# One decoder layer on one core: order of the late value rows, of the last one-hot batches and of four TensorE rows changed

## The reference, cut to what matters

```python
xs  = h.reshape(n_chunks, 128, D)          # two chunks of 128 tokens
idx = expert_idx.reshape(n_chunks, 128, K) # K = 8 heads * 16 experts of 128 * 128
u   = jnp.take(expert_u, ic, axis=0)
act = gelu(einsum('ckd,cd->ck', u, xc))
vv  = jnp.take(expert_v, ic, axis=0)
out = einsum('ck,ckd->cd', gc * act, vv)   # then h + out, and an RMS norm over D
```

## Time and profile before

| | us |
|---|---|
| median of 3 runs | 2041.2 (2039.21 to 2043.6) |
| the profiled execution, its own time | 2039.45 |
| its span, first to last instruction | 2037.5 |
| TensorE busy | 1788.4 (88%) |
| VectorE busy | 1368.4 (67%) |
| GpSimd busy | 1022.5 (50%) |
| ScalarE busy | 560.0 (27%) |

### The profile page before, as it was taken

One profiled execution on the slowest core, in us unless ns is written; L12 is line 12 of the kernel. 1 busy time (PEld: TensorE's weight loads), 2 busy tenths in 40 slices (PEclk: granted clock), 3 DMA queues, 4 the chain that ended last, 5 costly groups with the idle time before them and its releaser, 6 DMA issues.

```text
span 2037.5 us, 21513 instructions
## 1 busy us (share of the span) xinstructions
PE 1788.4 (88%) x7530; PEld 1188.6 (58%) x7531; DVE 1368.4 (67%) x2205; ACT 560.0 (27%) x1011; POOL 1022.5 (50%) x643
## 2 busy tenths in 40 slices
PE   7999999999999999765565578888877989999997
PEld 7998899888998898622222233444433544444442
DVE  4473453223324348899999988887888877888866
ACT  5334453345433520201010033223314620000001
POOL 4443343444332414566655554564555656777742
PEclk9999999999999999877777899999998999999998
DMA  8875454655546689999999999999999989999997
GB/s 208 239 174 147 141 184 155 197 190 186 167 145 198 194 287 399 344 421 418 417 418 415 410 402 398 402 416 402 404 417 401 397 302 403 385 410 378 397 421 318
DMA packets 157650, 647.41 MB, mean 318 GB/s; under 512 B 25894, under 2 KB 31086, under 8 KB 95598
## 3 DMA queue, kind: packets, MB, share of 16 engines
q0 software_dynamic: 73728, 450.98, 54.7%
q1 hardware_dynamic: 83824, 195.16, 29.5%
HBM read 729.91 MB, written 2.10 MB: 359 GB/s over the span
## 4 chain that ended last, share of the span: by engine, by line
PE 61%; DMA 18%; DVE 14%; issue 4%; POOL 2%; ACT 0%; DVEq 0%; POOLq 0%; SPq 0%; ACTq 0%
PE acc L1813 8%; PE misc L1813 8%; DMA u_ring<-in_peer_u_dram,idx 7%; DMA v_high<-in_peer_v_dram,idx 7%; PE acc L1469 5%; PE acc L1471 5%; PE acc L1470 5%; PE acc L1476 5%; PE acc L1477 5%; PE acc L1478 5%; DVE product L1314 5%; DVE product L1316 5%; PE misc L1778 4%; PE acc L1758 3%; DMA v_low<-in_peer_v_dram,idx 1%
## 5 line engine op out<-in xcount | busy, mean ns | idle before, releaser
L486 POOL TENSOR_TENSOR w_lo<-raw,w_hi 128x1024 fp32r<-128x1024 f32 x112 | 273.4, 2441 | 430.0 <-ACT w_hi L583 429.6
L1778 PE MATMUL misc<-v_high,diag 128*128 128x512 f32 x512 | 268.1, 673 | 104.9 <-DMA v_high<-in_peer_v_dram,idx 96.9
L1778 PE MATMUL misc<-v_low,diag 128*128 128x512 f32 x512 | 274.0, 688 | 93.5 <-DMA v_low<-in_peer_v_dram,idx 77.6
L583 ACT ACTIVATE w_hi<-raw 128x1024 fp32r<-128x1024 f32 x224 | 237.0, 1060 | 352.7 <-PE acc L1478 171.5
L910 DVE TENSOR_TENSOR w_lo<-raw,w_hi 128x1024 fp32r<-128x1024 f32 x112 | 149.3, 1334 | 266.1 <-ACT w_hi L583 266.0
L526 POOL DMA_INDIRECT u_ring<-in_peer_u_dram,idx x160 | 210.0, 1313 | 192.7 <-DVE dots L1316 136.5
L1469 PE MATMUL acc<-t_hi,w_hi 128*128 128x256 f32 x896 | 255.9, 286 | 0.0
L1470 PE MATMUL acc<-t_lo,w_hi 128*128 128x256 f32 x896 | 253.9, 283 | 0.0
L1471 PE MATMUL acc<-t_hi,w_lo 128*128 128x256 f32 x896 | 253.9, 283 | 0.0
L1778 PEld LDWEIGHTS misc<-v_low,diag 128*128 128x128 f32 x512 | 108.0, 220 | 249.7 <-issue 137.9
L1778 PEld LDWEIGHTS misc<-v_high,diag 128*128 128x128 f32 x512 | 105.2, 215 | 253.1 <-DMA v_high<-in_peer_v_dram,idx 133.0
(11 more groups left out here) (262 smaller groups left out, 2665.2 us busy)
## 6 DMA issues: line engine op xcount, KB each, us to landing
u_ring<-in_peer_v_dram SPq DMA_DIRECT2D x48, 1024.0 KB, 8.9
raw<-in_w_in_dram SPq DMA_DIRECT2D x64, 512.0 KB, 5.2
raw<-in_xattn_wk_dram SPq DMA_DIRECT2D x32, 512.0 KB, 4.8
raw<-in_xattn_wv_dram SPq DMA_DIRECT2D x32, 512.0 KB, 3.7
raw<-in_w_out_dram SPq DMA_DIRECT2D x32, 512.0 KB, 4.7
raw<-in_xattn_wq_dram SPq DMA_DIRECT2D x32, 512.0 KB, 4.6
raw<-in_xattn_wo_dram SPq DMA_DIRECT2D x32, 512.0 KB, 4.8
praw<-in_peer_wq_dram SPq DMA_DIRECT2D x24, 512.0 KB, 8.6
```

Of the source, the lines that this page charges most:

```text
L486: nc.gpsimd.tensor_tensor(w_lo[:, j % RING, :, :], raw[:, j % RING, :, :], w_hi[:, j % RING, :, :].bitcast(F32), ALU.subtract).then_inc(lo ...
L1778: ins = nc.tensor.matmul(o, diag[:, n % 4, :], v_slot(n % VS)[:, i * CW:(i + 1) * CW], start=False, stop=False)
```

## The change

Four edits. `LAST_K` lets the eight batches of groups 14 and 15 stand at k = 3, 4, 6, 7, 8, 10, 11, 12 (before: 3, 5, 7, 8, 10, 12, 14, 15). `LATE` is four higher: TensorE takes four late rows whole (117, 119, 121, 123; before six, 113 to 123), DVE two more; `first_sums` stays at m = 112, `gained(0)` and `scaled(0)` stand ahead of m = 114 and 115 (before ahead of 116 and 118, since 115 and 117 were TensorE's). The late slots come in the order 4, 6, 0, 1, 5, 2, 3, and slots 4, 5, 6 each wait for the last reader of what they overlie: dot 127, dot 255, dot 251. Value rows 126 and 127 leave groups 14/15's list on TensorE and follow dense tiles 0 and 1; ACT still makes their diagonals at their old places.

```diff
+        LAST_K = 11
-            return range(b + (k - 2) * 8 // 14, b + (k - 1) * 8 // 14)
+            return range(b + min((k - 2) * 8 // LAST_K, 8), b + min((k - 1) * 8 // LAST_K, 8))
-        LATE = TILE0 - TOP
+        LATE = TILE0 - TOP + 4
         def late_slot(m):
-            return (m + 4) % V2S
+            return (4, 6, 0, 1, 5, 2, 3)[m % V2S]
                 else:
-                    pool.wait_ge(dot_done, GROUPS * TOP)
+                    pool.wait_ge(dot_done, (PH * TOP, GROUPS * TOP, last_dot(6) + 1)[slot - VS])
-                if m == LATE:
+                if m == TILE0 - TOP:
                     first_sums()
-                if m == LATE + 3:
+                if m == TILE0 - TOP + 2:
                     gained(0)
-                if m == LATE + 5:
+                if m == TILE0 - TOP + 3:
                     scaled(0)
                     for n in share[taken(p, k):taken(p, k + 1)]:
-                        take_values(n)
+                        if n < TILE0 - 2:
+                            take_values(n)
                 if t < DENSE - 3:
                     dense_tile(t, 1).then_inc(tile_used, 1)
+                if t < 2:
+                    take_values(TILE0 - 2 + t)
```

## The result

| | before | after |
|---|---|---|
| median, us | 2041.2 (7 runs, 2038.87 to 2043.6) | 2050.17 (7 runs, 2047.21 to 2055.15) |
| profiled execution, us | 2039.45 | 2048.55 |
| its span, us | 2037.5 | 2046.4 |

The changed kernel is slower by 0.43%: ratio 1.0043, 95% interval 1.0034 to 1.0052. I had said 2041, no change, with a range to 2047. Two executions further down, one of e10 (2335.39 us) and one of e9 (2701.99 us), ran at a mean granted clock of 0.74 and 0.62 and are left out of the ratios, though not of the medians.

A forecast was written before the change was run, and what follows sets the result against it. The end was taken as bound by the arrival of all bytes, so by DMA idle time. 2039.45 + 1.3 (POOL's queue) - 1.4 (four rows) = 2039.35 for the profiled execution, 2041 as median; range 2034.5 to 2047.

The forecast's parts named there:

- The bound: Last 30 us: the end waits for all bytes to be in; TensorE's list has slack; idle DMA time counts.
- rival 2: POOL's requests m = 6 to 11 held behind row 127, no gain at the end: slower, 2046.8 us; chance 0.28.
- the term for POOL's queue: Late-row requests up to 1681: equal bytes, but the lagging DMA engine falls behind; +1.3 us, bounds 0.2 and 2.4.
- 14.6 against 14.6 MB: Bytes moved by 1681, late rows, tiles and 1.7 MB of others: the same after as before.
- my 1648: Start of dense tile 0 on TensorE, 12.1 us before 1660.15.
- a row 123 at low clock: TensorE's last late row before `take_sums`, if its clock has dropped: up to +2.7 us.
- Bounds 0 to +3 us, I take 0: Denser one-hot batches in group 14: ACT's extra work hidden by requests some 25 us ahead of landing; 0 us.
- my 1637.04: Time at which dense tile 0 is asked for, taken as in the kernel before.
- The four rows: Four late rows on TensorE instead of six: POOL's wait until 1999.62 goes; -1.4 us, bounds -3 to +2.7.
- The early requests: Late rows m = 0 to 3 asked for before 1640, filling the DMA engines' idle stretch.
- Rival 1: Hole in DMA filled and stays filled: four early rows, 6.5 us of transfer, reach the end; 2034.6 us; chance 0.28.
- Rival 3: One DMA engine is always last, so filling the others' idle time is worth nothing; 2042.2 us; chance 0.12.

The follow-up runs named there:

- e10: Kernel before with only value rows 126 and 127 moved behind dense tiles 0 and 1; 2047.14 us, ratio 1.0030.
- e9: Changed kernel with batches back at k = 3 to 15 and slots 2 and 3 coming at m = 10 and 11; 2041.81 us, ratio 1.0002.
- e2: Kernel before with only the denser one-hot batches; 2042.8 us, ratio 1.0001.
- e4: Kernel before with only the new slot order and the waits slot by slot; 2039.4 us, ratio 0.9994.
- e1: Changed kernel with the one-hot batches back at k = 3 to 15; 2047.15 us, ratio 1.0027.
- e5: Kernel before with only four late rows on TensorE instead of six; 2041.69 us, ratio 0.9992.
- e6: Kernel before with the new slot order and waits and four late rows on TensorE; 2038.87 us, ratio 0.9985.
- e3: Changed kernel with value rows 126 and 127 back in group 15's list, none between tiles; 2039.55 us, ratio 0.9990.
- e11: Changed kernel with batches at k = 3 to 13, only row 127 behind tile 0, slot 3 first used by m = 12; 2036.7 us, ratio 0.9977.

## Why the prediction was wrong

**The bound was right for the loss, not for the kernel before.** I read "the end is tied to the moment when all bytes are in; TensorE's list has slack near it" off two waits. But from 1700 on the chain of waits of the kernel before is TensorE's list (298.6 us of matmuls, and one tile's landing of 10.20 us at 1969.45). From there it goes through TensorE's first late row, for whose slot POOL stood still for 4.88 us, to the last rows:

```profile
1995.39 3.45 PE acc L1787 x8
...
1999.62 0.99 POOL v_more L533
...
2000.92 10.92 DMA v_last<-in_peer_v_dram,idx
...
2011.88 10.21 PE acc L1787 x16
```

So both bind there, within a few microseconds: in e2's profiled execution, 3.8 us of bytes behind, the chain from 1700 on goes through the transfers and no dense tile. Bytes that come earlier can gain little then (e4). In the changed kernel the bytes bind alone: only 5.8 us of matmuls are left in the chain from 1700 on, and TensorE waits 10.71 us for DMA after the last dense tile. Its first late row then takes 5.76 us instead of 3.60, at a mean granted clock of 0.62, between the two levels of 1.2 and 2.4 GHz:

```profile
2008.75 5.76 PE L1789 MATMUL acc<-v_high,diag 128*128 128x512 f32 x8 [10.71 <-DMA v_high<-in_peer_v_dram,idx]
...
2026.09 3.70 PE L1789 MATMUL acc<-v_more,diag 128*128 128x512 f32 x8 [1.26 <-DMA v_more<-in_peer_v_dram,idx]
```

**The mechanism was named, as rival 2, and its size missed.** The step that failed is the term for POOL's queue: "Bytes by 1681 ... 14.6 against 14.6 MB ... I take the middle, +1.3 us". By itself this edit measured 6.1 us, interval 3.9 to 8.4 (e10). Even with tile 0 at 1649.99, near my 1648, e1 moved 4.44 + 2.25 MB for POOL's queue and 3.15 + 2.10 MB of tiles from 1632 to 1681, 11.9 MB in place of my 14.6. Two things are in it. The requests for m = 5 and 6 came at 1663.48 and 1673.79 where I had 1660.6 and 1670.9: 3 us later, 1.2 MB. Of the other 1.5 MB about half is that I let the queue run full 1.6 us after m = 6's request: from 1673.79 to 1681 e1 moved 1.59 MB, where 5.6 us at 0.42 MB/us would be 2.4. The remainder I can't assign; I had counted every early late row at the mean 0.68 MB. Both ends of my term, 0.2 and 2.4, rest on the same times of the requests and on a queue that is full by 1681, so the range had no room for that error.

**What no term of the sum had.** Taken one at a time the four edits give 6.1 (e10) - 1.2 (e4) - 1.6 (e5) + 0.2 (e2) = 3.5 us. The changed kernel lost 8.8. The other 5.3 us come only in combination: 2.4 us when the two rows move with the new slots and the four rows in place (e1 against e6 is 0.0042, e10 0.0030), 2.2 more with the denser batches (0.0016 between e1 and after, where e3 against e6 has 0.0005), and the rest in smaller differences. With intervals of some 2 us on each ratio the sum is uncertain by about 4 us. How the edits act on each other stays open.

**Rival 2's number was near by luck.** Its condition, tile 0 at 1649 or later, was met in e1 (1649.99), and its 2046.8 is near e1's 2047.15. But 2.7 us of it are a row 123 at low clock, which ran in 3.70 us there (2022.87). Its price for the queue itself was 2.9 us, where e10 measured 6.1. The changed kernel's 2050.17 lies above the time of every rival.

**"Bounds 0 to +3 us, I take 0" for the denser batches.** By itself right: e2 is 1.0001. But the reason I gave, cover on ACT, was not what was used up: VectorE, whose list I had not counted, waited for TensorE to free the one-hot buffers, 12.1 us in three waits, and with it the dots. Tile 0 was asked for at 1647.25 for my 1637.04. With POOL held behind tiles 0 and 1 this delay moves both gaps, and the changed kernel is 0.0016 above e1; with the rows in the list the same batches cost 0.0005 (e3 against e6), which the intervals don't tell from none. That the two edits reinforce each other fits these numbers, but is not shown.

**The four rows: in line with the forecast.** -1.4 us forecast, -1.6 measured in e5, with an interval of -3.5 to +0.2, so that no gain is not excluded. The +2.7 of a row 123 at low clock did not come: it ran in 3.70 us, above.

**The early requests.** Rival 1's +6.5 us of bytes came true (e4: 5.2 us) and its 6.5 us of time did not (1.2). Rival 3 foresaw that filling the idle time is worth almost nothing, but its reason, one DMA engine that is always last, was not tested. TensorE's list as the chain in e4 explains it from the trace; no run parts the two. For it: in e11 TensorE waits 7.34 us for DMA after the last dense tile, so its list doesn't bind, and without the four rows' 1.6 us some 3.1 us are gained for 3.9 us of bytes. Against it: e3, where TensorE waits 4.03 us there, gained only some 0.4 us for 2.7 by the same count, and with four late rows on TensorE the requests are worth no more than without (e6 is 0.0007 below e5, with an uncertainty of twice that).

**Clock.** Tile 0's first half took 5.64 us after 3.20 us of idle time, as forecast, against 3.60 for the next (mean granted clock 0.63 and 1.00 of 2.4 GHz).

## What to carry to other kernels

When a buffer's last reader is moved behind long work, look not at that buffer but at the queue that will wait for it: everything behind the waiting request stops too, though its own buffers are free. Here 5.9 us of the loss (1.0043 to 1.0014) went when the same two slots were asked for five rows later, with the compute order unchanged. And a stretch in which the busiest engine shows 100% may be the very one that loses the time: compare the bytes moved from the start up to a common point. And follow the chain of waits to its end before saying what binds: a kernel can be bound by TensorE's list before an edit and by the transfers after it.

## What the runs showed of the hardware that I had not expected

Bytes that came late and bytes that came early did not count alike: 5.6 us of missing transfer cost 6.1 us (e10), while 5.2 us of transfer brought forward gave 1.2 (e4). Whether the transfers themselves or TensorE's list is the reason is open: in e4 the chain of waits ran through TensorE, and in e11, where it did not, 3.9 us brought forward gave 3.1 once the four rows' 1.6 are taken off, each with an uncertainty of 2 us or more.

And one profiled execution can lie well off its kernel's median: e6's had tile 0 asked for at 1644.22, where before it was 1637.04 with the same batches, and took 2045.1 us against a median of 2038.87. It had moved 2.8 MB (6.6 us) less by 1440, with the same work up to there. A single pair of profiles would have called the faster kernel the slower one.
